# Second block: the high operand of the projections alternates between two buffers and is made by chunks; the FFN takes its operand unnormed

## The reference, cut to what matters

```python
y_attn = dsa_attention(...).reshape(b, l, ATTN_WIDTH) @ w_attn_out[i]
y_conv = (cb * short_conv(cc * cu, conv_w[i])) @ w_conv_out[i]
mixed = jax.nn.sigmoid(ga) * y_attn + jax.nn.sigmoid(gb) * y_conv
h = h + mixed @ w_out[i]
f = rmsnorm_2(h, norm_ffn_g[i])          # h * rsqrt(mean(h*h) + EPS) * gain
h = h + (jax.nn.silu(f @ w_gate[i]) * (f @ w_up[i])) @ w_down[i]
```

## Time and profile before

| | |
|---|---|
| median of 3 runs | 1405.67 us (1405.59 to 1407.37) |
| the profiled execution's own time | 1406.31 us |
| its span, first to last instruction | 1404.6 us |
| TensorE matmuls busy | 1223.7 us, 87% |
| VectorE busy | 863.3 us, 61% |
| ScalarE busy | 664.5 us, 47% |
| mean granted TensorE clock | 0.982 |

### The profile page before, as it was taken

The page is one execution under the profiler, slowest core; times in us unless marked ns, Lnnn a source line. Parts: engine busy times, 40 slices in busy tenths (PEclk is TensorE's granted clock), DMA queues, the critical chain, the costliest instruction groups (busy, mean ns, idle before and its releaser), DMA issues.

```text
span 1404.6 us, 18989 instructions
## 1 busy us (share of the span) xinstructions
PE 1223.7 (87%) x6374; PEld 852.5 (61%) x6374; DVE 863.3 (61%) x1856; ACT 664.5 (47%) x1437; POOL 267.7 (19%) x301
## 2 busy tenths in 40 slices
PE   6999898887777878787777787999999989899998
PEld 4888785232222223332222223999999989899976
DVE  6753476666666667776666545477846656644454
ACT  4645445444444445554444434244435664433344
POOL 4000022433333333343333330000000020000000
PEclk9999989999999999999999999999999999999999
DMA  6331249999999999999999994345544345465553
GB/s 220 125 102 61 90 177 364 423 421 421 422 421 422 421 421 420 398 423 421 421 421 421 421 422 173 116 164 181 171 145 135 113 151 172 149 182 184 184 167 106
DMA packets 67353, 378.30 MB, mean 269 GB/s; under 512 B 7488, under 2 KB 7616, under 8 KB 34384
## 3 DMA queue, kind: packets, MB, share of 16 engines
q0 software_dynamic: 36864, 268.45, 46.1%
q1 hardware_dynamic: 30128, 107.85, 23.4%
q10 hardware_dynamic: 288, 1.08, 0.2%
HBM read 376.30 MB, written 1.05 MB: 269 GB/s over the span
## 4 chain that ended last, share of the span: by engine, by line
PE 51%; DMA 32%; DVE 7%; ACT 6%; issue 4%; DVEq 0%; SPq 0%; ACTq 0%
DMA work<-in_rows,work 32%; PE ps L526 28%; PE ps L872 7%; PE ps L935 4%; DVE w_lo L352 2%; PE ps L574 1%; ACT work L1310 1%; DVE work L1919 1%; PE ps L575 1%; PE ps L576 1%; ACT w_hi L344 1%; ACT work L1303 1%; ACT work L1306 1%; PE ps L763 1%; DVE work L2081 1%
## 5 line engine op out<-in xcount | busy, mean ns | idle before, releaser
L872 PE MATMUL ps<-work 128*128 128x512 f32 x1024 | 503.1, 623 | 130.5 <-ACT work L1310 130.2
L872 PEld LDWEIGHTS ps<-work 128*128 128x128 f32 x1024 | 180.6, 192 | 449.4 <-ACT work L1310 302.2
L1919 DVE CUSTOM_DVE_ANT_0 work<-work,ps 128x1024 f32<-128x1024 f32 x256 | 312.5, 1221 | 212.6 <-DMA work<-in_rows,work 211.2
L476 POOL DMA_INDIRECT work<-in_rows,work x256 | 242.4, 947 | 588.0 <-PE ps L872 396.4
L352 DVE TENSOR_TENSOR w_lo<-ring,w_hi 128x1024 fp32r<-128x1024 f32 x198 | 243.0, 1232 | 145.1 <-ACT w_hi L344 143.3
L526 PE MATMUL ps<-x_hi,w_hi 128*128 128x256 f32 (+2 forms) x1184 | 294.0, 290 | 13.1 <-ACT x_hi L362 6.7
L526 PE MATMUL ps<-x_lo,w_hi 128*128 128x256 f32 (+2 forms) x1240 | 302.3, 285 | 1.1 <-issue 1.1
L526 PEld LDWEIGHTS ps<-x_lo,w_hi 128*128 128x128 f32 x1240 | 236.2, 194 | 1.0 <-issue 0.6
L526 PEld LDWEIGHTS ps<-x_hi,w_hi 128*128 128x128 f32 x1184 | 224.0, 192 | 19.8 <-issue 10.3
L344 ACT ACTIVATE w_hi<-ring 128x1024 fp32r<-128x1024 f32 x198 | 205.8, 1052 | 58.6 <-PE ps L935 27.2
L1303 ACT ACTIVATE work<-work,peer_root 128x1 f32<-128x1 f32 x256 | 75.1, 293 | 316.1 <-DVE work L1919 315.9
(11 more groups left out here) (312 smaller groups left out, 1155.8 us busy)
## 6 DMA issues: line engine op xcount, KB each, us to landing
ring<-in_stream SPq DMA_DIRECT2D x198, 512.0 KB, 3.4
work<-in_rows,work POOLq DMA_INDIRECT x256, 14.8
res<-in_tokens SPq DMA_DIRECT2D x4, 272.0 KB, 3.6
gain_rows<-in_gain_rows SPq DMA_DIRECT2D x1, 1024.0 KB, 9.8
out_dram<-work SPq DMA_DIRECT2D x4, 256.0 KB, 2.3
work<-in_kiwi ACTq DMA_DIRECT2D x1, 544.0 KB, 3.5
work<-in_keys SPq DMA_DIRECT2D x1, 512.0 KB, 9.0
work<-in_gain ACTq DMA_DIRECT2D x1, 512.0 KB, 3.3
```

The lines of the kernel that those rows point to most:

```text
L476: g.indirect_dma_start(out=gathered[:, n % ROWS, :], out_offset=None, in_=rows_dram, in_offset=bass.IndirectOffsetOnAxis(ap=expert[:, n:n ...
L872: last = mm(ps[:, Y_BANK[t] + j, :], diag[:, n % DIAGS, :], gathered[:, n % ROWS, D + 512 * j:D + 512 * j + 512], start=False, stop=k == S ...
L1919: v.tensor_tensor_reduce(R["product"][:, D * (n % 2):D * (n % 2) + D], gathered[:, n % ROWS, 0:D], ps[:, bank:bank + 2, :].rearrange("p b ...
```

## The change

- The attention stage's operand goes to `x_peer`, early, while the convolution's tiles are still running from `x_hi`. Its low part goes to the shared `x_lo` once the last tile of the convolution, now low first, has read it.
- The out stage's operand goes to `x_hi` chunk by chunk, as the sums of the attention stage come. Its first tile is a chunked one: `first_query_block` is generalised to `chunked_block`. The low chunks are made by DVE, four before the last sum, four after it.
- The gate stage's operand is the residual times the gain, without the root, in `x_peer`, chunk by chunk, as the additions come. The first gate tile is a chunked one too. DVE multiplies every gate and up tile by the root; ACT takes the Silu from SBUF.
- The sum of squares comes after the first gate tile, and all of `open_sums` after the fourth.
- The weights are split one block further ahead from the attention stage on. The table with Ln and Exp is loaded at the head of the attention stage.
- The down stage's operand lies in slots of `x_hi` alone, high and low part side by side; ACT copies its first four chunks without waiting for the end of the gate stage.

```diff
@@ -263,9 +263,10 @@
+        up = ffa["up"].rearrange("p (n t) -> p n t", n=2)
@@ -324,14 +325,16 @@
+        gate_silu, hidden_ready = sem("gate_silu"), sem("hidden_ready")
...
-        X_CONV, X_ATTN, X_MIXED, X_FFN = X_MIX + 1, X_MIX + 2, X_MIX + 3, X_MIX + 4
-        HIDDEN0 = 2 * (X_FFN + 1)
+        X_CONV, X_ATTN = X_MIX + 1, X_MIX + 2
+        HIDDEN0 = 2 * (X_ATTN + 1)
+        AT_MIXED, AT_FFN = C, 2 * C
@@ -388,7 +390,7 @@
         def norm_bank(k):
...
-            return 2 if k else 7
+            return 4 if k else 7
...
         def bank_of(g):
@@ -804,26 +806,26 @@
-            def first_query_block():
+            def chunked_block(b0, g0, parts, at):
...
-                    pe.wait_ge(peer_hi, c + 1)
+                    pe.wait_ge(peer_hi, at + c + 1)
...
-                    pe.wait_ge(peer_lo, c + 1)
+                    pe.wait_ge(peer_lo, at + c + 1)
...
@@ -928,11 +930,11 @@
-                at = k * REAL + P * t
+                hi, lo = (x_hi[:, at:at + P] for at in (2 * k * REAL + P * t, (2 * k + 1) * REAL + P * t))
...
-                for x, w in ((x_hi, w_hi), (x_hi, w_lo), (x_lo, w_hi)):
+                for x, w in ((hi, w_hi), (hi, w_lo), (lo, w_hi)):
@@ -1031,13 +1033,23 @@
-                column_block(FIRST["w_conv_out_2"] + n, TILE0["w_conv_out_2"] + n, REAL)
-            columns("w_attn_out_2", REAL, X_ATTN)
-            columns("w_out_2", REAL, X_MIXED)
-            open_sums(range(0, 6))
+                column_block(FIRST["w_conv_out_2"] + n, TILE0["w_conv_out_2"] + n, REAL, low_first=n == 7)
+            for n in range(8):
+                column_block(FIRST["w_attn_out_2"] + n, TILE0["w_attn_out_2"] + n, REAL,
+                             operand=X_ATTN if n == 0 else None, parts=peer_x, low_first=n == 7)
+            chunked_block(FIRST["w_out_2"], TILE0["w_out_2"], x_parts[REAL], AT_MIXED)
+            for n in range(1, 8):
+                column_block(FIRST["w_out_2"] + n, TILE0["w_out_2"] + n, REAL, low_first=n == 7)
+            b0, g0 = FIRST["w_gate_up_2"], TILE0["w_gate_up_2"]
+            chunked_block(b0, g0, peer_x, AT_FFN)
...
-            open_sums(range(6, 8))
-            columns("w_gate_up_2", REAL, X_FFN)
+            for n in range(1, RING):
+                column_block(b0 + n, g0 + n, REAL, parts=peer_x)
+            pe.wait_ge(root_ready, 2)
+            open_sums(range(8))
+            with pe.Fori(1, 2 * FF // RING) as i:
+                for k in range(RING):
+                    column_block(b0 + k, g0 + k, REAL, i, i, parts=peer_x)
             b0, turns = FIRST["w_down_2"], FF // RING
             with pe.Fori(0, turns) as i:
@@ -1069,7 +1081,8 @@
             def root(k):
...
-                nc.scalar.preload_act_table_set("natural_log_exp_and_others")
+                if k == 0:
+                    nc.scalar.preload_act_table_set("natural_log_exp_and_others")
@@ -1473,33 +1486,37 @@
-            tiles_are_taken(act, TILE0["w_attn_out_2"])
-            operand_hi(act, X_ATTN, ya, None, 0)
+                elif n == 4:
+                    act.wait_ge(attn_taken, 4)
+                    operand_hi(act, X_ATTN, ya, None, 0, parts=peer_x)
+            nc.scalar.preload_act_table_set("natural_log_exp_and_others")
+            b = FIRST["w_attn_out_2"] + 2
+            split_hi(act, b)
             for n in range(8):
-                ahead(FIRST["w_attn_out_2"] + n)
-            act.wait_ge(tile_ready, TILE0["w_out_2"])
-            operand_hi(act, X_MIXED, ya, mixed_ready, 1)
+                split_hi(act, b + n + 1)
+                act.wait_ge(mixed_ready, n + 1)
+                a(x_parts[REAL][0][:, n, :], ya[:, n, :], ACT.Copy).then_inc(peer_hi, 1)
+            b, gain_at = FIRST["w_out_2"] + 3, SMALL["norm_ffn"][0]
             for n in range(8):
-                ahead(FIRST["w_out_2"] + n)
+                split_hi(act, b + n)
+                tile_is_taken(act, TILE0["w_out_2"] + n)
+                a(peer_x[0][:, n, :], res[:, n, META:], ACT.Copy,
+                  scale=small[:, gain_at + n:gain_at + n + 1]).then_inc(peer_hi, 1)
                 if n % 2:
-                    tile_is_taken(act, TILE0["w_out_2"] + n - 1)
-                    tile_is_taken(act, TILE0["w_out_2"] + n)
...
-            operand_hi(act, X_FFN, tokens_of(sq_late, REAL), normed, 3)
             b0, g0 = FIRST["w_gate_up_2"], TILE0["w_gate_up_2"]
...
             def gate_tiles(turn=None):
...
-                    ahead(b0 + k, t)
+                    if k or turn is not None:
+                        ahead(b0 + k, t)
...
-                        act.wait_ge(tile_ready, t * RING + (g + 1))
-                        if turn is not None:
-                            act.wait_ge(tile_taken[BANK[g + 2]], t + ORD[g + 2])
-                        a(sg[:, k, :], bank_of(g)[:, 0:REAL], ACT.Silu).then_inc(tile_taken[BANK[g]], 1)
+                        act.wait_ge(tile_taken[BANK[g]], t + (ORD[g] + 1))
+                        a(sg[:, k, :], sg[:, k, :], ACT.Silu).then_inc(gate_silu, 1)
@@ -1510,12 +1527,15 @@
-                a(x_hi[:, k * REAL:(k + 1) * REAL], src, ACT.Copy).then_inc(x_hi_ready, 1)
-            tiles_are_taken(act, g0 + 2 * FF)
+                a(x_hi[:, 2 * k * REAL:(2 * k + 1) * REAL], src, ACT.Copy).then_inc(x_hi_ready, 1)
+            b0 = FIRST["w_down_2"]
+            for k in range(RING):
+                act.wait_ge(hidden_ready, k + 1)
+                row_operand(hidden[:, k, :], b0 + k)
+            act.wait_ge(hidden_ready, FF)
...
-            b0 = FIRST["w_down_2"]
-            with act.Fori(0, FF // RING) as i:
+            with act.Fori(1, FF // RING) as i:
@@ -2115,10 +2135,24 @@
             for n in range(8):
                 ahead(FIRST["w_conv_out_2"] + n)
-            operand_lo(dve, X_ATTN, ya)
+            dve.wait_ge(mix_lo_read, 2)
+            operand_lo(dve, X_ATTN, ya, parts=peer_x)
...
+            def mixed_lo_2(c):
+                dve.wait_ge(peer_hi, AT_MIXED + c + 1)
+                tt(x_parts[REAL][1][:, c, :], ya[:, c, :], x_parts[REAL][0][:, c, :].bitcast(F32),
+                   ALU.subtract).then_inc(peer_lo, 1)
+            b = FIRST["w_attn_out_2"] + 2
+            split_lo(dve, b)
             for n in range(8):
-                ahead(FIRST["w_attn_out_2"] + n)
+                split_lo(dve, b + n + 1)
+                if n == 7:
+                    dve.wait_ge(mix_lo_read, 3)
+                    for c in range(4):
+                        mixed_lo_2(c)
@@ -2126,34 +2160,64 @@
-                i = tt(ya[:, n, :], yc[:, n, :], yco[:, n, :], ALU.add)
-                if n % 4 == 3:
-                    i.then_inc(mixed_ready, 1)
-            operand_lo(dve, X_MIXED, ya)
+                tt(ya[:, n, :], yc[:, n, :], yco[:, n, :], ALU.add).then_inc(mixed_ready, 1)
+            for c in range(4, C):
+                dve.wait_ge(mixed_ready, c + 1)
+                mixed_lo_2(c)
+            gain_at = SMALL["norm_ffn"][0]
+            def ffn_lo(c):
+                dve.wait_ge(peer_hi, AT_FFN + c + 1)
+                stt(peer_x[1][:, c, :], res[:, c, META:], small[:, gain_at + c:gain_at + c + 1],
+                    peer_x[0][:, c, :].bitcast(F32), ALU.mult, ALU.subtract).then_inc(peer_lo, 1)
+            b = FIRST["w_out_2"] + 3
             for n in range(8):
-                ahead(FIRST["w_out_2"] + n)
+                split_lo(dve, b + n)
+                if n == 7:
+                    dve.wait_ge(mix_lo_read, 4)
+                    for c in range(4):
+                        ffn_lo(c)
...
-                if n % 2 == 0 and n:
+                if n in (4, 6):
...
+            for c in range(4, C):
+                ffn_lo(c)
+            fold(1, tokens_of(sq_late, REAL), 0)
...
-            norm(1, res[:, :, META:], "norm_ffn", tokens_of(sq_late, REAL))
-            operand_lo(dve, X_FFN, tokens_of(sq_late, REAL))
             b0, g0 = FIRST["w_gate_up_2"], TILE0["w_gate_up_2"]
-            with dve.Fori(0, FF // 2) as i:
+            dve.wait_ge(root_ready, 2)
+            def hidden_tiles(turn=None):
+                i = 0 if turn is None else turn
...
-                    ahead(b0 + k, i)
+                    if k or turn is not None:
+                        ahead(b0 + k, i)
+                    g = g0 + k
+                    if k < 2 and turn is not None:
+                        dve.wait_ge(hidden_ready, i * 2 + (k - 1))
+                    dve.wait_ge(tile_ready, i * RING + (g + 1))
+                    tt(sg[:, k, :] if k < 2 else up[:, k - 2, :], bank_of(g)[:, 0:REAL], rstd[:, 0:REAL],
+                       ALU.mult).then_inc(tile_taken[BANK[g]], 1)
...
-                        g = g0 + k
-                        dve.wait_ge(tile_taken[BANK[g - 2]], i + (ORD[g - 2] + 1))
-                        dve.wait_ge(tile_ready, i * RING + (g + 1))
-                        tt(hidden[:, i * 2 + (k - 2), :], bank_of(g)[:, 0:REAL], sg[:, k - 2, :],
```

(28 more changed lines are left out.)

20 lines of the change are left out of this document (10 added, 10 removed).

## The result

The changed kernel takes 1410.17 us (median of 20 runs, 1406.88 to 1412.38), the kernel before 1407.48 (20 runs, 1404.65 to 1410.97). The ratio is 1.0022, 95% interval 1.0013 to 1.0030: 3.1 us slower, 1.8 to 4.2. The forecast was +1.2 us (1406.9). The measured time lies within its range of 1402.9 to 1411.0, near the upper end. So the two traces stand 5.5 us apart, and 2.9 of that belongs to these two executions.

The account below looks back on a forecast made before the run. TensorE was taken to set the time, so only its waits, some 15 us, could be won. Gate start +0.2, identity products +3.6, cold clock +1.7 and down stage -4.2 gave +1.2 us: 1406.9 us, range 1402.9 to 1411.0.

Parts of the forecast that it names:

- The ring eats the prize: Attention stage: ACT and DVE queues wait on each other in a circle, 3.40 us against TensorE's 2.88; chance 0.65.
- full prize: Rival, second block's stage boundaries: ACT and DVE keep TensorE's pace, -14.2 us, 1391.5 us; chance 0.07.
- Sum 0 at 1151.78: Attention stage: DVE's first chunk sum, after table load, splits and gating, comes at 1151.78 us.
- Sum 0 to 7: Attention stage: DVE's chunk sums 3.40 us apart, the last also behind four low chunks, at 1176.94.
- Addition 0 to 1: Out stage: first two residual additions at 1179.88 and 1182.96, the second later if out tile 1 runs cold.
- Addition 1 to 7: Out stage: residual additions in steps of 3.60 and 3.08 take 21.62 us, against 17.3 of TensorE.
- Addition 7 to gate tile 2's last group: Gate stage: gate tile 1 starts 3.65 us after the last addition, then one cold-clock spell of 1.7 us.
- The identity products: Gate stage: done before gate tile 1 in the old kernel, now still to come there: +3.6 us.
- Down: Down projection: TensorE starts at 1334.33 instead of 1336.86, 2.5 us saved, plus 1.7 of cold block: -4.2 us.
- Costs put at nothing: Gate and up tiles: root multiplications, 1.7 us of DVE per four tiles, and Silu from SBUF hidden; multiplications uncovered 18.7 us.
- Table switch: Rival, head of the attention stage's loop: the table load also drains, 1.4 us later, sum +2.6, 1408.3 us; chance 0.03.
- the clock decide: Rival, out, gate and down stages: cold clock adds up to 4.9 us, 1411.8 in full; decides past +2.8; chance 0.25.

Follow-up runs that it names:

- sums_early: Changed kernel with 24 of 32 identity products ahead of gate tile 0, the other 8 after gate tile 3, no filler products: 1405.54 us, 0.9991 of before.
- fill: Changed kernel with unread matmuls put into TensorE's waits in out tile 0 and gate tile 0: 1406.26 us, 0.9991 of before.
- both_open: Changed kernel with DVE's low split moved behind the sum in the attention stage and behind the addition in the out stage: 1396.32 us, 0.9911 of before.
- after_again: The changed kernel unaltered, run once more: 1410.17 us, 1.0015 of before.
- attn_open: Changed kernel with DVE's low split put behind the sum in the attention stage only: 1398.74 us, 0.9933 of before.
- dose: Changed kernel with one more unread ACT copy in each turn of the attention stage's chunk loop: 1410.86 us, 1.0030 of before.
- down_only: Kernel before with only the FFN operand moved to the other buffer and the down stage's operand prepared early: 1402.34 us, 0.9955 of before.
- out_open: Changed kernel with DVE's low split put behind the addition in the out stage only: 1404.78 us, 0.9979 of before.
- both_open_2: Second run of the changed kernel with DVE's low split moved back in both attention and out stage: 1394.65 us, 0.9911 of before.
- both_open_sig: Changed kernel with DVE's low split moved in both stages, and conv tile 5's weights split ahead of the long Sigmoid: 1392.75 us, 0.9898 of before.

## Why the prediction was right, and where its size was off

- **The ring eats the prize: right, and shown.** Predicted period 3.40, measured 3.45; undone, the gain appears. With both rings open 12.5 us of the full prize's 14.2 come by the ratios, 11.6 by the stretches. Of what is missing there, the waits left at the norm (0.7), at the operand's low half (0.2) and at the down stage (1.7, where the bound counted 1.4) make about half; the rest is not accounted for. The 0.05 in the period is nearly all the copy: it takes 0.32 to the next instruction, where the forecast took 0.28 from a copy out of PSUM.
- **Sum 0 at 1151.78:** measured 1153.37, when the 0.74 us by which this execution was already late at convolution tile 5 (1138.09 against 1137.35) is taken off. 1.5 of the 1.6 is the cold clock in tile 5: it was taken 4.67 us after its start, not 3.17 as in the earlier trace rows. The forecast took one trace's warm tile for the rule.
- **Sum 0 to 7:** predicted 25.16, measured 25.50. **To addition 0:** 2.94 and 3.00.
- **Addition 0 to 1:** 3.88 with the 0.8 that I took for the clock, measured 4.44. The window above shows the clock down for 10 us, not for one spell of 6.8. **Addition 1 to 7:** 21.62 and 21.80.
- **Addition 7 to gate tile 2's last group:** with one cold spell of 1.7 this was to take 10.15, measured 10.72: the spell cost 2.3. The identity products cost the 3.6: gate tiles 3 and 4 start their last groups 6.44 apart (1222.45 and 1228.89), 2.88 without them. Of that price 2.7 was avoidable: sums_early shows that it is the order, not the work.
- **Down:** predicted -4.2. From gate tile 4's last group to the first down product it is 115.09 us and was 117.41, so 2.3 earlier (2.5), and the rest from there to the end takes 66.12 in place of 67.74, as the first block is warm, 1.6: -3.9. TensorE began 1.61 after the last take, not 1.28: VectorE's steps from the take to the product and from there to the low part took 0.65 and 0.48 us (forecast 0.46 and 0.34). The idle time was 1.65, not 1.4.
- **Costs put at nothing:** VectorE has 74.31 us from 1209 to 1333 where it had 60.34, the multiplications by the root, and the full-clock part of the stage keeps its 2.88 us a tile. Nothing of it reached the end.
- **Table switch:** the load at the ring's head shows 1.28 us and the next instruction 1.29 after its start, as in the earlier trace rows. By the drain that the Trainium skill states (ScalarE: Activation LUTs, What ACT_TABLE_LOAD costs) ScalarE would have stood 1.4 longer; this row shows no such gap.

Timeline of ScalarE of after, head of the ring:

```profile
1148.92 1.28 ACT L1492 ACT_TABLE_LOAD   x1
1150.21 2.01 ACT L347 ACTIVATE w_hi<-ring 128x1024 fp32r<-128x1024 f32 x2
```

The term that was sized worst is the clock. In the two traces the differences from the forecast are 1.6 + 0.3 + 0.1 + 0.6 + 0.2 + 0.6 + 0.3 = 3.7, of which 2.7 are clock (tile 5, out tile 1, gate); with the forecast's 1.2 they give 4.9, close to the 4.8 by which the stretches differ. But the 1.5 of tile 5 is chance of these two executions at least in part. Without it the stretches differ by 3.3, close to the measured 3.1, and the forecast is short by some 2.2: 1.2 of clock, 0.7 of longer steps, 0.3 at the down stage.

So the mechanism was right, and the size was right only as far as the wide range goes. The +3.1 lies just past the +2.8 from which on the forecast let the clock decide, a case that it gave 0.25, and its sign for that case, more than 7 us at 0.50 in all, was met: the three spells of after last some 20 us. That rival was thus partly true. It did not turn a gain into a loss by itself, since with the clock kept (fill, 0.9991) there is still no gain that can be told from zero; but it made the difference between that and a loss that can be measured. The spells in the out and gate stages are themselves the ring's doing: both_open, without fillers, keeps 1.00 from 1143 to 1229. What decides is the ring.

What stays open: why the wait of 2.23 us at convolution tile 5 is followed by a cold spell in some executions and not in others, and with it how much of the difference between before and after is chance there.

## What to carry to other kernels

When a change lets one in-order engine feed another chunk by chunk, write down the order of both queues and look for a closed circle: copy, high split, low split, sum, and back to the copy. If the circle's period (here 3.45 us) is longer than the pace of the engine that it feeds (2.88), the gain is lost however idle both engines look, and moving the instruction that waits behind the one that need not wait gives it back (some 15 us here, in two loops). Then look at where the fed engine waits, and put there the work that stood elsewhere (4 us here, about half of it by keeping the clock up).

## What the runs showed of the hardware

- TensorE's clock stayed at its lower level for about 10 us while it was fed in drips: waits of 2.3, 2.0 and 0.55 us with two to four products between. With 34 unread products a chunked tile it stayed at 1.00.
- The same wait of 2.23 us was followed by a cold spell in after, after_again, attn_open, both_open, dose, down_only, fill and sums_early, and by none in before, out_open and both_open_2. A spell there cost 1.5 us.
- Two low halves of 128x1024 took 2.90 us on VectorE while GpSimd worked on an addition beside them, and 2.36 in the kernel before (at 1147.86, when GpSimd had just ended its addition). After's timelines of VectorE and of GpSimd:

```profile
1148.14 2.90 DVE L372 TENSOR_TENSOR x_lo<-work,x_peer 128x1024 fp32r<-128x1024 f32 x2
```

```profile
1148.98 0.98 POOL L492 TENSOR_TENSOR work<-work 128x256 f32<-128x256 f32 x1 [2.14 <-ACT work L1094]
```

The GpSimd addition took 0.98 in place of 0.74, so both were slowed where they overlapped. The rows fit one engine standing still while the other works: GpSimd 0.24 longer behind the first half, then VectorE's second half late by 0.54. It made TensorE wait 0.2 us at the second half (0.6 in both_open_sig, where GpSimd's addition starts 0.41 behind VectorE's first half and not 0.84). The Trainium skill, SBUF — State Buffer, SBUF: two separate sides, says that an instruction of VectorE with two SBUF inputs and one of GpSimd that reads SBUF exclude each other for a whole instruction; by that rule, the trace agrees.
